# Sums of squares for six norms: GpSimd adds the tiles first, TensorE multiplies with ones only at the end

## The reference, cut to what matters

```python
def rmsnorm(h, g):
    hf = h.astype(jnp.float32)
    hf = hf * lax.rsqrt(jnp.mean(hf * hf, axis=-1, keepdims=True) + NORM_EPS)
    return (hf * g.astype(jnp.float32)).astype(h.dtype)
...
        x = x + g1x * fourier_mix(hx, fnet_wo[fi], fnet_bo[fi])
...
        hx = rmsnorm(x, norm_g[i, 1]) * (1.0 + sc2x) + sh2x
        x = x + g2x * ec_moe(hx, moe_router[i], moe_wg[i], moe_wu[i], moe_wd[i])
...
        x = x + mixed @ w_out[l]
        h2 = rms_norm(x, norm2[l])
        x = x + jnp.square(jax.nn.relu(h2 @ w_up[l])) @ w_down[l]
    return rms_norm(x, final_norm)
```

## Time and profile before

| | |
|---|---|
| time, median of 3 runs | 4384.12 us (4383.26 to 4389.61) |
| the profiled execution: its time, its span | 4399.33 us, 4397.5 us |
| TensorE busy (matmuls) | 3938.0 us, 90% of the span |
| VectorE, ScalarE, GpSimd busy | 1677.7, 851.6, 614.9 us |
| mean granted clock of TensorE | 0.958 of 2.4 GHz |

### The profile page before, as it was taken

The page is one execution under the profiler, slowest core; times in us unless marked ns, Lnnn a source line. Parts: engine busy times, 40 slices in busy tenths (PEclk is TensorE's granted clock), DMA queues, the critical chain, the costliest instruction groups (busy, mean ns, idle before and its releaser), DMA issues.

```text
span 4397.5 us, 93458 instructions
## 1 busy us (share of the span) xinstructions
PE 3938.0 (90%) x40040; PEld 2527.7 (57%) x40040; DVE 1677.7 (38%) x3445; ACT 851.6 (19%) x1847; POOL 614.9 (14%) x603
## 2 busy tenths in 40 slices
PE   4979999989967777777889998999999989999998
PEld 4534444445556766666444444447688854658887
DVE  2423112154444554544132112453345424515453
ACT  2100000020144444444110001115000011420000
POOL 4000000000022222222000000000234300003342
PEclk8989999999989999999889999999999999999999
DMA  8277887852200000000359996110122221102221
GB/s 329 96 294 302 336 333 296 335 222 83 80 8 13 13 13 13 13 15 14 134 244 429 429 428 274 58 58 1 58 96 77 77 84 39 39 20 79 94 77 39
DMA packets 54240, 619.72 MB, mean 141 GB/s; under 512 B 5648, under 2 KB 8976, under 8 KB 18320
## 3 DMA queue, kind: packets, MB, share of 16 engines
q1 hardware_dynamic: 49664, 599.41, 34.5%
q10 hardware_dynamic: 2448, 9.05, 0.6%
q0 software_dynamic: 1792, 6.29, 0.4%
HBM read 602.40 MB, written 12.32 MB: 140 GB/s over the span
## 4 chain that ended last, share of the span: by engine, by line
PE 70%; issue 15%; DMA 5%; DVE 5%; ACT 1%; DVEq 1%; PEld 1%; PEldq 0%; SPq 0%; POOLq 0%; POOL 0%; ACTq 0%
PE bank L890 57%; PE bank L1353 12%; DMA ring<-slabs 2%; DMA work<-slabs 2%; PEld bank L890 1%; DMA kv<-work 1%; PE bank L1400 1%; DVE hx L2389 0%; PEldq L1797 0%; DVE work L3091 0%; DVE work L2694 0%; DVE work L2374 0%; DVE work L2365 0%; DVE work L3110 0%; DVE hc L2434 0%
## 5 line engine op out<-in xcount | busy, mean ns | idle before, releaser
L890 PE MATMUL bank<-ring,work 128*32 128x256 f32 (+3 forms) x7002 | 763.7, 439 | 69.5 <-DMA ring<-slabs 57.7
L890 PE MATMUL bank<-work 128*128 128x256 f32 (+8 forms) x3590 | 786.5, 429 | 25.3 <-DVE work L3091 15.9
L890 PEld LDWEIGHTS bank<-work 128*128 128x128 f32 (+3 forms) x3590 | 500.2, 184 | 298.5 <-issue 217.3
L890 PEld LDWEIGHTS bank<-ring,work 128*32 128x32 f32 (+2 forms) x7002 | 317.4, 124 | 490.8 <-issue 393.3
L890 PE MATMUL bank<-work,ring 128*128 128x256 f32 (+1 forms) x1616 | 482.9, 457 | 13.4 <-DVE work L3110 5.1
L890 PE MATMUL bank<-hx,ring 128*128 128x512 f32 (+1 forms) x1344 | 486.3, 517 | 6.5 <-DVE hx L2389 4.5
L1353 PE MATMUL bank<-work 64*64 64x64 f32 x11520 | 338.4, 235 | 119.6 <-issue 82.6
L890 PEld LDWEIGHTS bank<-work,ring 128*128 128x128 f32 x1616 | 307.2, 191 | 183.1 <-issue 134.5
L1353 PEld LDWEIGHTS bank<-work 64*64 64x64 f32 x11520 | 309.4, 146 | 155.0 <-issue 151.7
L890 PEld LDWEIGHTS bank<-hx,ring 128*128 128x128 f32 x1344 | 257.0, 192 | 222.0 <-issue 201.0
L3228 POOL TENSOR_TENSOR work<-ring 128x512 f32<-128x512 f32 (+1 forms) x48 | 78.7, 1639 | 1931.5 <-DVE resc L3079 1482.3
(11 more groups left out here) (311 smaller groups left out, 4517.1 us busy)
## 6 DMA issues: line engine op xcount, KB each, us to landing
ring<-slabs SPq DMA_DIRECT2D x228, 2048.0 KB, 9.7
work<-slabs SPq DMA_DIRECT2D x48, 2048.0 KB, 18.3
work<-kv SPq DMA_DIRECT2D x18, 384.0 KB, 3.1
kv<-work SPq DMA_DIRECT2D x2, 3072.0 KB, 15.7
kv<-work ACTq DMA_DIRECT2D x6, 512.0 KB, 16.7
work<-tabs ACTq DMA_DIRECT2D x1, 2176.0 KB, 8.4
resx<-xT SPq DMA_DIRECT2D x1, 2048.0 KB, 11.0
outT<-hx ACTq DMA_DIRECT2D x8, 256.0 KB, 2.1
```

Of the source, the lines that this page charges most:

```text
L890: return pe.matmul(out, lhsT, rhs, start=(k == 0), stop=(k == n - 1))
```

## The change

In these four places GpSimd adds the squares of tiles 1 to 6 into tile 0 (`squares_summed`), tile by tile as ScalarE makes them, and raises a new semaphore `squares_added`. TensorE does nothing about squares until its last projection or block is issued. Then it multiplies ones with tile 0, which now holds seven tiles (`added_squares`), and with tile 7 (`last_squares`). In the feed-forward part GpSimd adds tiles 1 to 5 in the last three blocks, behind its own `sums`, and TensorE then takes the added tile and tiles 6 and 7. The two other norms of the kernel that lie behind the mixtures of experts keep `square_sum`.

For the two kinds of `dense_summed` the sum is moved from bank 0 to bank 7. The projection then turns through 7 banks (`me.width = 7`), and its eighth output tile takes bank 0 again, after a wait for VectorE's first addition.

```diff
+            def added_squares(n, parts):
+                pe.wait_ge(squares_added, n)
+                for sq, b, cols in parts:
+                    mm(b[:, 0:cols], ones, sq[:, 0, 0:cols], 0, 2)
+            def last_squares(tiles, parts):
+                for k in tiles:
+                    pe.wait_ge(norm_act, me.t["na"].at(k + 1))
+                    for sq, b, cols in parts:
+                        m = pe.matmul(b[:, 0:cols], ones, sq[:, k, 0:cols], start=False, stop=(k == KT - 1))
+                m.then_inc(norm_pe, me.add("np"))
+                me.t["na"].n += KT
...
-                            pe.wait_ge(drained, me.reused())
+                            pe.wait_ge(*(again or (drained, me.reused())))
...
-            def dense_summed(segs, parts):
-                def lagged(j):
-                    if 4 * half + j:
-                        square_sum(4 * half + j - 1, parts)
+            def dense_summed(segs, parts, n):
                 for half in range(2):
-                    dense(segs, then=lagged)
-                square_sum(KT - 1, parts)
+                    dense(segs, again=(norm_dve, me.t["nd"].at(1)))
+                added_squares(n, parts)
+                last_squares([KT - 1], parts)
...
-                if f:
-                    square_sum(f - 1, [(sqx, P[6], NX), (sqc, P[7], NC)])
-            square_sum(KT - 1, [(sqx, P[6], NX), (sqc, P[7], NC)])
+            added_squares(1, [(sqx, P[6], NX), (sqc, P[7], NC)])
+            last_squares([KT - 1], [(sqx, P[6], NX), (sqc, P[7], NC)])
...
-            dense_summed([(Rx[:, 1:KT + 1, :], NX)], [(sqx3, P[0], NX)])
+            me.width = 7
+            dense_summed([(Rx[:, 1:KT + 1, :], NX)], [(sqx3, P[7], NX)], 2)
+            me.width = 8
...
-                dense_summed([(OT, NX)], [(sq2, P[0], NX)])
+                me.width = 7
+                dense_summed([(OT, NX)], [(sq2, P[7], NX)], l * 2 + 3)
+                me.width = 8
...
-                        def tiles_summed():
-                            for k in (2 * j - 2, 2 * j - 1):
-                                square_sum(k, [(hx, P[7], NX)])
...
-                for k in (KT - 2, KT - 1):
-                    square_sum(k, [(hx, P[7], NX)])
+                added_squares(l * 2 + 4, [(hx, P[7], NX)])
+                last_squares([KT - 2, KT - 1], [(hx, P[7], NX)])
...
+            def squares_summed(tiles, parts):
+                for k in tiles:
+                    if k > 1:
+                        pool.drain()
+                    pool.wait_ge(norm_act, me.t["na"].at(k + 1))
+                    for sq in parts:
+                        m = pool.tensor_tensor(sq[:, 0, :], sq[:, 0, :], sq[:, k, :], ALU.add)
+                return m
+            me.t["na"].n = 1 + 2 * KT
+            squares_summed(range(1, KT - 1), [sqx, sqc]).then_inc(squares_added, 1)
...
+            me.t["na"].n = 3 * (1 + 2 * KT)
+            squares_summed(range(1, KT - 1), [sqx3]).then_inc(squares_added, 1)
...
             with me.loop("layer", 2) as l:
                 me.t["slab"].n += 8
+                me.t["na"].n += 1
+                squares_summed(range(1, KT - 1), [sq2]).then_inc(squares_added, 1)
+                me.t["na"].n += KT + 1
...
                         sums(down_weights(w), *sum_down)
+                        if c and j:
+                            m = squares_summed([k for k in (2 * j - 2, 2 * j - 1) if k], [hx])
+                m.then_inc(squares_added, 1)
+                me.t["na"].n += KT
```

More of the change, by code:

```diff
@@ L421, in build @@
         norm_dve, norm_act, norm_pe, norm_pool = (sem(n) for n in ("norm_dve", "norm_act", "norm_pe", "norm_pool"))
+        squares_added = sem("squares_added")
         late_summed, late_copied, late_turned, late_placed, late_ready = (sem(n) for n in ("late_summed", "late_copied", "late_turned", "late_placed", "late_ready"))
@@ L916, in transposed, with dense @@
                 m.then_inc(filled, me.add("filled"))
-            def dense(segs, first=None, then=None):
+            def dense(segs, first=None, again=None):
                 pe.wait_ge(slab_loaded[me.slot()], me.landed())
@@ L1825, in _, with block_of @@
                 pe.wait_ge(drained, me.first_bank())
-                def block_of(n, a, sums, b, ready=None, turned=None, made=None, between=None, last=True):
+                def block_of(n, a, sums, b, ready=None, turned=None, made=None, last=True):
                     def term(name, left, right, each=None):
@@ L1855, in block_of @@
                     term("p5", sums[0], b["t1"])
-                    if between:
-                        between()
                     summed(3)
@@ L1884, in rows_ready @@
                             return lambda k: pe.wait_ge(ff_made, l * 48 + (24 * c + 3 * k + 1 + second))
-                        def tiles_summed():
-                            for k in (2 * j - 2, 2 * j - 1):
-                                square_sum(k, [(hx, P[7], NX)])
-                        block_of(12 * c + 8 + j, down_weights(w), sum_down, rows_b, ready=rows_ready if j == 0 else None, made=l * 48 + (24 * c + 24) if j == 0 else None,
-                                 between=tiles_summed if c and j else None)
-                for k in (KT - 2, KT - 1):
-                    square_sum(k, [(hx, P[7], NX)])
+                        block_of(12 * c + 8 + j, down_weights(w), sum_down, rows_b, ready=rows_ready if j == 0 else None, made=l * 48 + (24 * c + 24) if j == 0 else None)
+                added_squares(l * 2 + 4, [(hx, P[7], NX)])
+                last_squares([KT - 2, KT - 1], [(hx, P[7], NX)])
                 me.t["nd"].n += KT
@@ L2207, in _ @@
             tile_squares([(resx, sqx3)])
-            root(rstd, [(P[0], NX)])
+            root(rstd, [(P[7], NX)])
             act.wait_ge(late_ready, 2)
@@ L2333, in _ @@
                 tile_squares([(resx, sq2)])
-                root(rstd2, [(P[0], NX)])
+                root(rstd2, [(P[7], NX)])
                 me.t["nd"].n += KT
```

3 lines of the change are left out of this document (1 added, 2 removed).

## The result

| | before | after |
|---|---|---|
| time, median of 6 runs | 4384.43 us (4383.26 to 4389.61) | 4337.80 us (4328.70 to 4349.23) |
| ratio, 95% interval | | 0.9894 (0.9877 to 0.9910) |
| profiled execution: time, span | 4399.33, 4397.5 us | 4341.01, 4339.2 us |
| TensorE busy, entries | 3938.0 us, x40040 | 3897.5 us, x39960 |

The change makes the kernel 46.6 us faster, 1.06%. The question is where the other 13 us came from.

A forecast was written before the change was run, and what follows sets the result against it. TensorE was taken to set the pace in all changed stretches; savings of 7.7, 15.5 and 10.3 us, together 33.5, from the median of 4384.1 gave 4350.6 us. Its own range was 4345 to 4356, widened to 4343 to 4364.

The forecast's parts named there:

- TensorE sets the pace, and a product taken out gives its own length: Fourier, RWKV and attention outputs and feed-forward parts: TensorE never pauses there, so removed products save their own length, 33.5 us.
- the five later norms: RWKV output and two attention outputs, 15.5 us, and two feed-forward parts, 10.3 us, saved by removed products.
- the sum: Savings of 7.7 us in the Fourier output, 15.5 in three projections and 10.3 in two feed-forward parts, together 33.5.
- The added sum takes tile 6's slot, or falls into the pause: The added product costs nothing: in projections it replaces tile 6's, in feed-forward ends it fits into 4.83 us of idling.
- the clock gain at the feed-forward ends: If TensorE's clock stayed up in the shortened pause, 1.9 us more per end; counted as nothing, 3.8 in the range.
- GpSimd keeps up: At the changed norms, additions of 1.27 us stay hidden, with nearly 5 us of slack at a projection's end.
- the slower rival: GpSimd's additions run behind the last projection or block, so TensorE waits: 4404 us in the middle, chance 3%.
- that of exclusion at the ends: GpSimd and VectorE exclude each other at six ends, 1.27 us each, 7.6 us lost: 4358.2 us, chance 5%.
- Transfers move up with the work: Loads and token-row writes, in the experts' stages too, are released by work that moves, so no gain returns as waits.
- Nothing here is on a schedule of its own: Whole kernel: loads wait for TensorE's release and move up with it, so the full 33.5 us is saved.
- 5.2 due: Saving of one projection output, here an attention output: six sums of squares of 0.86 us taken from TensorE.

The follow-up runs named there:

- e4: Changed kernel, with GpSimd's Fourier weight additions waiting until VectorE has scaled ctx: 4332.48 us, ratio 0.9884 to the kernel before.
- e3: Kernel before, with GpSimd's Fourier weight additions waiting until VectorE has scaled ctx: 4376.72 us, ratio 0.9980 to the kernel before.
- e10: e4 with 12 one-row, one-column products added at TensorE's start: 4350.29 us, ratio 0.9912 to the kernel before.
- e2: Changed kernel again, unchanged: 4330.79 us, ratio 0.9886 to the kernel before.
- The ordered pair: e3 and e4, the kernels before and after with GpSimd's Fourier weight additions waiting for VectorE: 4376.72 and 4332.48 us.
- e1: Kernel before again, unchanged: 4385.24 us, ratio 1.0006 to the kernel before.
- E5: e3 with the Fourier part of the change only: 4364.68 us, ratio 0.9951 to the kernel before.
- e6: e4 with the Fourier norm put back as before: 4360.56 us, ratio 0.9947 to the kernel before.
- e14: e4 with 12 one-column products behind the last norm of the program: 4336.27 us, ratio 0.9879 to the kernel before.

## Why the prediction was right, and where not

- **TensorE sets the pace, and a product taken out gives its own length**: right in the traces. Tiles 6.22 us apart (6.21), blocks 24.17 us (24.17), no squares between projections. In the total the five later norms, 25.8 us by the sum, gave 27.5 at one placement and 14.5 at another; at equal clock 20 and 18. So the near match of 27.5 is in part luck of the clock.
- **The added sum takes tile 6's slot, or falls into the pause**: right; the pause was to be about 4.0 us and is 3.98. Of the clock gain at the feed-forward ends little came: the two products take 3.54 us where 3.78 were, at a granted 0.64 in the microsecond in which they start. The clock of the whole run is another matter: the six runs of after have 0.9637 on the mean, against 0.9612, worth some 7 us by the estimate above, and the prediction had 3.8 at most.
- **GpSimd keeps up**: right. 1.26 us an addition (1.27), 1.95 a pair (2.1 with the drain), 4.2 us of slack (nearly 5). TensorE never waited for it at an added sum, so the slower rival and that of exclusion at the ends are out.
- **Transfers move up with the work**: right; the stretch of the first experts kept its length within 0.5 us and that of the second lost nothing, so none of the gain was given back as a wait in the first pair of profiles. (In e4 the first experts took 5.3 us more than in e3; e4 keeps its gain all the same.)
- **"Nothing here is on a schedule of its own", so 33.5 us from the median are the whole of it**: this step failed. The sum puts every stage that the change doesn't touch at nothing, and the only reason given is that the transfers move up. Two things outside the sum changed. One is the race in the Fourier stage, which costs before some 9 us at the median (5 at equal clock) and after nothing; it was visible in the trace of before as scalings of 4.6 us, and I read the earlier trace rows for the shape of such a collision without asking whether one lay on the path. The other is the placement of the scan's code, which the prediction did not have at all: 11 to 12 us, by putting 12 products back at no cost (e10), or 8 at equal clock.
- **The size.** 33.5 + 12 for the placement + 9 for the race is 54 us, where the runs have 46.6 and (in e2) 50. At equal clock 33.5 + 8 + 5 is 47, where the runs have 41 and (in e2) 44. Within the intervals both close; neither closes to the microsecond, and each adds up to a few us too many. The ordered pair has no race: 33.5 + 12 = 45.5, measured 44.2. Ordered and at before's placement, e10 against e3: 0.0068 of 4384, 30 us (27 at equal clock), for a sum of 33.5.

Left open: at equal clock the five later norms gave 20 and 18 us for a sum of 25.8, which only the first interval just reaches. Where the rest went is partly seen. The attention of layer 2 gave 1.2, 3.5 and 1.7 us in the three pairs of profiles (before and after, e1 and e2, e3 and e4), of 5.2 due; that of layer 1 gave 6.7, 6.4 and 4.2. E5 and e6, which looked far too small beside e3 and e4 (27 us of 44), give 12 and 18 at equal clock, together 30 of 36, and that agrees within the intervals. And why a set of boundaries costs more than another isn't settled, nor whether it moves the clock.

## What to carry to other kernels

Where a stage's pace is set by TensorE, a product moved off it shortens the stretch by its own length, and an idle GpSimd at 1.3 us per 128x512 addition is a good place for it. In straight code with short instructions, an edit ahead of a stage can move the time of the kernel by some 10 us without touching that stage (8 to 15 at equal clock, here in a scan of 800 us): before explaining a fraction of a per cent, put as many free instructions back as the edit took out, or try a few paddings at the start, which here gave the fastest version (0.9863 and 0.9865). Compare the granted clock of the runs too, before a difference of 10 us is given to the code. And look for instructions of VectorE that take ten times their usual length while GpSimd works, before trusting one profile's total.

## What the hardware showed that I had not expected

- TensorE's issue pauses once in 256 instructions of its stream, at a median of some 0.95 us in the scan (2.7 us at most in the profile of after), 149 to 166 us of the scan's 800. They go on at the same position up to the RWKV norm (12 boundaries, 0.92 us on the mean in the profile of after, 0.97 before). In the first experts' stage the same position shows a mean of 0.02 to 0.17 us and in the later stages, with larger products and in part in loops, it doesn't stand out.
- Two of VectorE's scalings, held for 4.6 us each, cost nothing at the end, while the third and fourth made TensorE wait 9.84 us and the Fourier output start 12 us later.
- The scan took 798 and 818 us in two executions with the same placement (e4, e14). TensorE idled 178.8 us in both; the difference is its busy time, at a granted clock of 0.97 and 0.94. A single profile doesn't settle 8 us.
